# Forgetting attention: causal triangle added on GpSimd, query blocks taken from last to first, weight splits moved to odd steps

## What is computed

```
q = rms_norm(q, q_g);  k = rms_norm(k, k_g)              # 8 heads of 64
c = cumsum(log_sigmoid(f_logit), axis=1)
s = (q @ k^T) / sqrt(64) + c[query] - c[key]
s = where(key <= query, s, -inf);  p = softmax(s)        # per head, per block of 128 queries
out = p @ v
pooled[g] = window mean of u[g] over the last 2, 4, 8 or 16 tokens;  y[g] = (pooled[g] - u[g]) @ w_pool[g] * scale
mix = concat(out, y) @ w_out
```

## Time and profile before

| | |
|---|---|
| median of three runs | 1791.82 us (1791.68 to 1792.4) |
| the profiled execution, its own time | 1791.34 us |
| its span, first to last instruction | 1789.5 us |
| mean granted TensorE clock (share of 2.4 GHz) | 0.991 |
| TensorE busy, matmuls | 1726.2 us, 96% |
| VectorE busy | 1176.4 us, 66% |
| ScalarE busy | 894.1 us, 50% |
| GpSimd busy | 201.5 us, 11% |
| the attention stage, first scores to last values | 708.3 to 837.3 us of the span |

### The profile page before, as it was taken

One profiled execution on the slowest core, in us unless ns is written; L12 is line 12 of the kernel. 1 busy time (PEld: TensorE's weight loads), 2 busy tenths in 40 slices (PEclk: granted clock), 3 DMA queues, 4 the chain that ended last, 5 costly groups with the idle time before them and its releaser, 6 DMA issues.

```text
span 1789.5 us, 25773 instructions
## 1 busy us (share of the span) xinstructions
PE 1726.2 (96%) x8602; PEld 1356.3 (76%) x8602; DVE 1176.4 (66%) x1809; ACT 894.1 (50%) x1319; POOL 201.5 (11%) x209
## 2 busy tenths in 40 slices
PE   6999989999999979999999999999998999999999
PEld 5777767788888757667788888887774788888887
DVE  6777775798989763555577777225796477777422
ACT  4466653688887733665344444124664444444310
POOL 0000000133333100001000000001991000000000
PEclk9999999999999979999999999999999999999999
DMA  9533124999999552111233223332661223333331
GB/s 394 206 95 105 61 80 139 355 358 383 386 382 385 197 199 91 60 60 57 76 102 95 94 94 101 123 94 61 164 157 49 83 95 94 94 97 101 119 94 59
DMA packets 78709, 270.02 MB, mean 151 GB/s; under 512 B 10983, under 2 KB 11239, under 8 KB 77360
## 3 DMA queue, kind: packets, MB, share of 16 engines
q1 hardware_dynamic: 74176, 260.96, 42.9%
q0 software_dynamic: 4464, 8.14, 1.2%
HBM read 256.02 MB, written 12.60 MB: 150 GB/s over the span
## 4 chain that ended last, share of the span: by engine, by line
PE 88%; DVE 4%; ACT 3%; DMA 3%; issue 2%; SPq 0%; POOL 0%; POOLq 0%; ACTq 0%; DVEq 0%
PE ps L1097 20%; PE ps L1099 19%; PE ps L1098 19%; PE ps L1365 3%; PE ps L1366 3%; PE ps L1367 3%; PE ps L1159 2%; PE ps L1387 2%; PE ps L1385 2%; PE ps L1386 2%; PE ps L1180 1%; PE ps L1739 1%; DMA raw<-in_w_a 1%; PE ps L1061 1%; PE ps L1118 1%
## 5 line engine op out<-in xcount | busy, mean ns | idle before, releaser
L1097 PE MATMUL ps<-h_hi,w_hi 128*128 128x512 f32 x1120 | 445.3, 398 | 2.1 <-DVEq L2366 1.2
L1099 PE MATMUL ps<-h_hi,w_lo 128*128 128x512 f32 x1120 | 437.0, 390 | 0.0
L1098 PE MATMUL ps<-h_lo,w_hi 128*128 128x512 f32 x1120 | 436.5, 390 | 0.0
L135 DVE TENSOR_TENSOR w_lo<-raw,w_hi 128x1024 fp32r<-128x1024 f32 x212 | 269.6, 1273 | 172.5 <-ACT w_hi L130 172.3
L130 ACT ACTIVATE w_hi<-raw 128x1024 fp32r<-128x1024 f32 x212 | 222.3, 1050 | 194.9 <-PE ps L1099 157.6
L1097 PEld LDWEIGHTS ps<-h_hi,w_hi 128*128 128x128 f32 x1120 | 210.4, 188 | 71.7 <-issue 28.6
L1099 PEld LDWEIGHTS ps<-h_hi,w_lo 128*128 128x128 f32 x1120 | 210.3, 188 | 44.5
L1098 PEld LDWEIGHTS ps<-h_lo,w_hi 128*128 128x128 f32 x1120 | 210.5, 188 | 41.8 <-issue 0.5
L175 DVE TENSOR_TENSOR w_lo<-ring,w_hi 128x1024 fp32r<-128x1024 f32 x128 | 149.6, 1218 | 26.8 <-ACT w_hi L171 26.8
L984 ACT ACTIVATE tmp<-ps,param 128x512 f32<-128x512 f32 x88 | 68.7, 780 | 184.9 <-DVE ps L2332 184.9
L2340 DVE SCALAR_TENSOR_TENSOR tmp<-ps,param,tmp 128x511 f32<-128x511 f32 (+1 forms) x176 | 131.8, 749 | 17.5 <-DVE tmp L2340 3.1
(11 more groups left out here) (351 smaller groups left out, 2740.9 us busy)
## 6 DMA issues: line engine op xcount, KB each, us to landing
ring<-in_w_m SPq DMA_DIRECT2D x192, 512.0 KB, 6.3
raw<-in_w_b SPq DMA_DIRECT2D x180, 512.0 KB, 3.5
raw<-in_w_a SPq DMA_DIRECT2D x32, 512.0 KB, 3.7
ada_late<-in_ada_b SPq DMA_DIRECT2D x32, 512.0 KB, 4.6
ada<-in_ada_a SPq DMA_DIRECT2D x8, 1024.0 KB, 20.9
shifted<-glu SPq DMA_DIRECT2D x24, 260.0 KB, 4.8
y_tok<-y_dram SPq DMA_DIRECT2D x8, 512.0 KB, 7.3
x<-in_x SPq DMA_DIRECT2D x2, 1024.0 KB, 6.7
```

The source lines that it names most:

```text
L135: dve.tensor_tensor(self.lo[:, s, :], self.raw[:, s, :], self.hi[:, s, :].bitcast(F32), ALU.subtract).then_inc(self.lo_done, 1)
L1097: pe.matmul(dst, hi, a_hi, start=first, stop=False, skip_group_check=True)
L1098: pe.matmul(dst, hi, a_lo, start=False, stop=False, skip_group_check=True)
L1099: return pe.matmul(dst, lo, a_hi, start=False, stop=last, skip_group_check=True)
```

## The change

- The causal triangle is no longer a matmul. GpSimd adds it to `nck` in place, by a 128x128 addition per step (`masked(g)`), into the columns of the diagonal block. For this the query blocks go from 3 down to 0: a block's triangle may stay in `nck`, since later blocks don't read those columns. `masked(g)` waits until VectorE has read the same head's `nck` two steps earlier, or for the load of `nck`; `g_biased(g)` waits for `masked(g)`.
- GpSimd's window sums are put between the masks (`WINDOW_AFTER`).
- ScalarE's weight splits go from t = 0, 2, 6 to the ends of t = 1, 3, 5, those of VectorE from t = 1, 3, 7 to t = 2, 4, 6.
- `ln_qk` of q goes from ahead of the exponential of its iteration to behind it; `pooled_hi`, `evict_u`, `mix` and the last `pooled` move by a place or a step.
- In `OUT_EARLY` the 28 early parts of the output product are spread otherwise.

```diff
-             26: ((2, 0), (2, 1), (0, 6), (1, 6)), 27: ((2, 6), (0, 2), (1, 2), (2, 2)),
-             28: ((3, 4), (3, 5), (3, 0), (3, 1)), 29: ((0, 7), (1, 7), (2, 7), (3, 6)), 30: ((3, 2), (3, 7))}
+             26: ((2, 0), (2, 1), (0, 6)), 27: ((1, 6), (2, 6), (0, 2), (1, 2)), 28: ((2, 2), (0, 7), (1, 7)),
+             29: ((2, 7), (3, 4), (3, 5), (3, 0)), 30: ((3, 1), (3, 6), (3, 2), (3, 7))}
+WINDOW_AFTER = {3: ((0, 0),), 9: ((1, 0), (1, 1)), 17: ((2, 0), (2, 1)), 18: ((2, 2),), 25: ((3, 0), (3, 1)), 26: ((3, 2), (3, 3))}
...
         def head_step(g):
-            return g // 8, g % 2, g % 8 // 2
+            return g // 8, g % 2, NT - 1 - g % 8 // 2
+
+        def pair_step(both):
+            return both // NT, NT - 1 - both % NT
...
             for g in range(GSTEPS):
                 i, t = g // 8, g % 8
                 more = i + 1 < H // 2
-                if t == 0 and 0 < i:
-                    pooled_hi(i - 1)
                 if t == 2 and more:
                     square_qk(i + 1, 1)
-                    ln_qk(i + 1, 0)
                 if t == 4 and more:
                     exp_qk(i + 1, 0)
                     exp_qk(i + 1, 1)
                 if g + 2 < GSTEPS:
                     g_exps(g + 2)
-                if t == 0:
-                    sb_.split_hi(act, 0, 10 + 3 * i)
-                    if more:
-                        square_qk(i + 1, 0)
+                if t == 0 and 0 < i:
+                    pooled_hi(i - 1)
+                if t == 0 and more:
+                    square_qk(i + 1, 0)
                 if t == 2 and more:
-                    sb_.split_hi(act, 0, 11 + 3 * i)
+                    ln_qk(i + 1, 0)
                 if t == 3 and more:
                     ln_qk(i + 1, 1)
-                if t == 6 and more:
-                    evict_u(i + 1)
-                    sb_.split_hi(act, 0, 12 + 3 * i)
-                if g == 26:
+                if g == 27:
                     pooled_hi(3)
-                if g % 2:
+                if t % 2:
                     g_out_hi(g // 2)
                 if g + 1 < GSTEPS:
                     g_turned(g + 1)
+                if t == 1:
+                    sb_.split_hi(act, 0, 10 + 3 * i)
+                if t == 3 and more:
+                    sb_.split_hi(act, 0, 11 + 3 * i)
+                if t == 5 and more:
+                    sb_.split_hi(act, 0, 12 + 3 * i)
+                if t == 6 and more:
+                    evict_u(i + 1)
...
-                              start=True, stop=False, skip_group_check=True)
-                for j in range(2):
-                    pe.matmul(ps[:, 2 * j, q * P:(q + 1) * P], C("ident"), C("causal"), start=False, stop=True,
-                              skip_group_check=True).then_inc(g_s, 1)
+                              start=True, stop=True, skip_group_check=True).then_inc(g_s, 1)
...
-                if h == 0:
-                    dve.wait_ge(g_nck, 1)
-                elif q == 0:
-                    dve.wait_ge(c_spread[h % 4], 48 + 16 * (h // 4 + (h % 4 > 0)))
+                dve.wait_ge(g_masked, g + 1)
                 dve.wait_ge(g_s, g + 1)
...
-                if t == 1:
+                if t == 2:
                     sb_.split_lo(dve, 0, 10 + 3 * i)
-                if t == 3 and more:
+                if t == 4 and more:
                     sb_.split_lo(dve, 0, 11 + 3 * i)
-                if t == 7 and more:
+                if t == 6 and more:
                     sb_.split_lo(dve, 0, 12 + 3 * i)
-                for at, pool in ((2, 0), (10, 1), (18, 2), (24, 3)):
+                for at, pool in ((2, 0), (11, 1), (19, 2), (26, 3)):
...
+            def masked(g):
+
+                i, j, q = head_step(g)
+                h, cols = 2 * i + j, slice(q * P, (q + 1) * P)
+                if q < NT - 1:
+                    pool.wait_ge(g_free, g - 1)
+                elif h == 0:
+                    pool.wait_ge(g_nck, 1)
+                else:
+                    pool.wait_ge(c_spread[h % 4], 48 + 16 * (h // 4 + (h % 4 > 0)))
+                pool.tensor_tensor(nck[:, h % 4, cols], nck[:, h % 4, cols], C("causal"), ALU.add).then_inc(g_masked, 1)
+
+            for g in range(GSTEPS):
+                masked(g)
+                for w, d in WINDOW_AFTER[g] if g in WINDOW_AFTER else ():
+                    window(w, d)
```

More of the change, by code:

```diff
@@ L442, in build @@
         win_step, mix_step, mixed_done, pool_mm = sems("win_step mix_step mixed_done pool_mm")
-        g_ck, g_nck, g_s, g_free, g_nm, g_exp, g_r, g_p = sems(
-            "g_ck g_nck g_s g_free g_nm g_exp g_r g_p")
+        g_nck, g_s, g_free, g_nm, g_exp, g_r, g_p, g_masked = sems(
+            "g_nck g_s g_free g_nm g_exp g_r g_p g_masked")
+        g_ck = sel_done
         g_tr, g_pt, g_o, g_hi, g_lo = sems("g_tr g_pt g_o g_hi g_lo")
@@ L453, in build @@
         pe_taps = sem("pe_taps")
-        taps_in, blocks_done = w2_in, sel_done
+        taps_in, blocks_done = w2_in, g_ck
         shifted_in = [sem(f"shifted_in{p}") for p in range(2)]
@@ L893, in first_neg_c @@
             def first_neg_c():
-                act.wait_ge(g_ck, 1)
+                act.wait_ge(g_ck, 1 + 1)
                 act.activation(nck[:, 0], ps[:, 0], ACT.Copy).then_inc(g_nck, 1)
@@ L912, in g_out_hi @@
             def g_out_hi(both):
-                i, q = both // NT, both % NT
+                i, q = pair_step(both)
                 act.wait_ge(g_o, both + 1)
@@ L1548, in g_scores @@
             def g_scores(both):
-                i, q = both // NT, both % NT
-                if q == 0:
+                i, q = pair_step(both)
+                if q == NT - 1:
                     pe.wait_ge(qk_new, 2 * i + 2)
@@ L1735, in taps @@
                 pe.wait_ge(sq_done, q + (MEAN * KC - 1))
-                pe.wait_ge(blocks_done, 1 + (2 if last else 1))
+                pe.wait_ge(blocks_done, 1 + 1 + (2 if last else 1))
                 for n in range(sets):
@@ L2257, in g_out_lo @@
             def g_out_lo(both):
-                i, cols = both // NT, slice(both % NT * P, (both % NT + 1) * P)
+                i, q = pair_step(both)
+                cols = slice(q * P, (q + 1) * P)
                 dve.wait_ge(g_hi, both + 1)
@@ L2564, in window @@
                    .then_inc(win_step, 1)
-            for g in range(NG):
-                for d in range(g + 1):
-                    window(g, d)
+            def masked(g):
[12 more added lines that the diff above has]
+                    window(w, d)
             pool.wait_ge(x_new, 5 * KC)
```

## The result

| | before | after |
|---|---|---|
| median | 1792.11 us (1791.68 to 1793.94, 4 runs) | 1807.33 us (1803.81 to 1807.77, 4 runs) |
| the profiled execution: its time, its span | 1791.34, 1789.5 us | 1807.77, 1806.0 us |
| mean granted TensorE clock | 0.991 | 0.984 |
| the stage, first scores to last values | 129.0 us | 141.2 us |
| GpSimd busy | 201.5 us | 221.4 us |

The changed kernel is slower: 1.0077 times the one before, 95% interval 1.0061 to 1.0093. The forecast was slower too, by 5.5 us; measured are 15.2. The time, 1807.3, lies outside the range of 1789.5 to 1801.5.

The account below looks back on a forecast made before the run. It took TensorE to bound the stage nearly everywhere, with waits for ScalarE in a burst. Burst waits +14.8, causal matmuls -9.0, last copy -0.3 gave +5.5 us: 1796.8, or 1797.3 against the median; range 1789.5 to 1801.5.

Parts of the forecast that it names:

- Reading of the bound: Stage of the change: bound by TensorE nearly everywhere, with short waits for ScalarE within t = 2 to 5.
- First half of the burst: In t = 2, k's `mean_square` waits for q's logarithm 2.6 us instead of 0.17, in three pairs.
- Second half: From that `mean_square` to the next pair's scores, TensorE waits 4.0 us instead of 1.49, in three pairs.
- Table loads: ScalarE's table loads on the two chains: 1.30 us each from the trace, not the skill's 2.66.
- Masks at nothing: GpSimd's 32 masks, 0.35 us each, cost nothing, covered by one query block of distance.
- the collision: Rival: masks and `at_nm` collide on the chains, 0.7 us a pair more, 1799.4, at worst 1805.7; chance 0.12.
- Causal matmuls: Sixteen pairs of causal matmuls removed from TensorE at 0.56 us each, 9.0 us saved, up to 11.4.
- The clock: Rival: waits lower TensorE's granted clock; one pair at 1.2 GHz costs near 28 us, 1825; chance 0.03.
- the end of the stage: TensorE's last wait, for the copy of transposed blocks, now one instead of four: 0.3 us shorter.

Follow-up runs that it names:

- splits_back: The changed kernel with ScalarE's and VectorE's weight splits back in their old iterations, q's logarithm still behind the exponential; 1793.61 us.
- filled: The changed kernel with matmuls that nobody reads put into TensorE's waits; 1800.41 us.
- masks_only: The changed kernel with weight splits and q's logarithm back in their old places, keeping masks, reversed blocks and small moves; 1787.61 us.
- lo_late: The changed kernel with VectorE's split of the middle weight chunk moved from t = 4 to t = 5; 1799.69 us.
- two_loads_2: masks_only with both logarithms in t = 2, exponentials behind them, splits later except in the third pair; two table loads a pair; 1790.77 us.

## Why the prediction was wrong

- **Reading of the bound: right.** TensorE's stage with short waits on ScalarE in t = 2 to 5; the change hit those.
- **First half of the burst: right.** 2.6 us forecast, 2.38 measured, in three pairs. The forecast took `at_nm` to be there by then; that was so, but only behind the split (splits_back).
- **Second half: right in one pair of three,** 4.0 forecast against 4.07 in the second pair, at the three places named, and 2.87 and 2.53 in the others. Part of that gap is the slow clock's (filled, above). All the waits grew by 12.3 us, of which 1.1 is a wait for a window sum in the last pair that I hadn't named; forecast were 14.8.
- **Table loads: the row was the right price.** 1.28 us and 0.01 to the logarithm. By the Trainium skill, ScalarE: Activation LUTs, "What ACT_TABLE_LOAD costs", with its drain of about 1.38 us, the first wait would by estimate be above 3.7 us; the measured 2.38 decides against it.
- **Masks at nothing: right,** 0.46 us each where I took 0.35, and the collision cost no time that the runs can tell. The Trainium skill, SBUF — State Buffer, "Who interferes with whom", describes the block, and `at_nm` at 0.514 against 0.220 us agrees.
- **Causal matmuls: mis-sized.** "The causal pair costs 0.56 us": 9.0 us forecast, 6.1 measured, 0.38 a pair. I took it as the rest of an iteration, and that rest also held the start of the filling behind: its first matmul takes 0.31 us to the next (771.35 to 771.66) and not 0.2275, and 0.34 in masks_only, where no causal pair is ahead. From start to start the pair takes 0.47 us in that iteration; what brings the mean down to 0.38 I can't place. A term made as a difference should take the start costs of its neighbours from a row. And this gain is only worth its size where TensorE is the bound.
- **The clock: the step that failed.** The rival had the right mechanism, but I gave it 0.03, saw only a whole pair at half clock (28 us) and left it out of the range. What came is in between: a few microseconds at 1.2 GHz after the waits in each of three pairs, 5.95 us more busy time in all, where the sum had 0. The earlier trace rows showed 0.86 and 0.50 as values of single stretches; I should have priced the clock by such stretches behind each group of waits, not by pairs, and put them into the range.

By the stage: 5.5 + 2.9 (causal) - 2.5 (waits) + 5.95 (clock) + 0.3 is 12.2. The 0.3 is the end of the stage: its wait did get shorter, 0.37 against 0.69 us, but that is in the waits already. Two misses nearly cancel here by luck: the causal matmuls brought 2.9 us less than forecast, the waits cost 2.5 us less. The further 3 us of the median lie outside the stage and are open.

## What to carry to other kernels

Where an engine that is 95% busy has a few iterations without slack, moving a 1 us instruction of another engine into them can cost its length per turn, whatever the average says (1.15 us in lo_late), or nothing, where it covers another wait (0.80 of 0.95 us in splits_back); write down both chains and put such instructions where the filling is thick. Price a wait of TensorE at more than its length: here 12.3 us of new waits came with 6 us more busy time from the clock, and matmuls that nobody reads, put into the waits, kept the clock up and made the stage 3.7 us shorter. And take a bundle apart before judging it: the masks and the new order were one change, one worth -5 us by itself and the other +16. They don't add up, for with the new order the masks bring 1 us at most that can be seen.

## What the runs showed that was not expected

- The clock fell for some microseconds at a time and not after each wait. In both of the first two pairs `mean_square` waited 2.38 us; behind it the clock was 0.70 and 0.87 (732 to 740) in the first, and 1.00 in the second, though TensorE had been busy for only 1.62 of 4 us. There it fell at the next group of waits. With the waits of masks_only, up to 0.95 us each, it never fell; with those of splits_back (2.34 and 0.77) it did, right behind the long one: `mean_square` took 1.72 us in place of 1.10. And length alone doesn't decide: in the third pair of two_loads_2 TensorE waited 0.95, 2.07 and 1.53 us within 11 us, and the clock stayed at 1.00.
- In the second pair of lo_late the clock was 0.80 and 0.77 right behind the first wait (764 to 772), and the 0.87 us that after waits for the transposes of step 5 was gone. It looks as if slower filling had covered that wait, and filled, with the clock at 1.00 and that wait in all three pairs, bears it out; no run slows the filling alone. It is a reason to split a stage's time within one kernel, as above, and not to add up effects of several.
